# Which weight units of an expert pass stay unsplit, and what the first three prepared units are

## The reference, cut to what matters

```python
def moe_swiglu(h, w_router, w1, w3, w2):
    logits = (h @ w_router).astype(jnp.float32)
    top_logit, top_idx = lax.top_k(logits, TOP_K)      # TOP_K = 2
    gates = jax.nn.softmax(top_logit, axis=-1)
    ...
        return (jax.nn.silu(xblk @ w1[e]) * (xblk @ w3[e])) @ w2[e]
    ...
    return jnp.zeros_like(h).at[tok].add(yb * gate[:, None])
```

## Time and profile before

| | us |
|---|---|
| median of 3 runs | 2702.24 (2699.02 to 2707.3) |
| the profiled execution's own time | 2699.6 |
| its span, first to last instruction | 2697.8 |
| TensorE busy | 2603.4 (97%) |
| TensorE weight load busy | 2052.8 (76%) |
| VectorE busy | 1822.9 (68%) |
| ScalarE busy | 1437.6 (53%) |
| mean granted TensorE clock | 0.988 of full |

### The profile page before, as it was taken

One profiled execution on the slowest core, in us unless ns is written; L12 is line 12 of the kernel. 1 busy time (PEld: TensorE's weight loads), 2 busy tenths in 40 slices (PEclk: granted clock), 3 DMA queues, 4 the chain that ended last, 5 costly groups with the idle time before them and its releaser, 6 DMA issues.

```text
span 2697.8 us, 47127 instructions
## 1 busy us (share of the span) xinstructions
PE 2603.4 (97%) x18358; PEld 2052.8 (76%) x18358; DVE 1822.9 (68%) x2625; ACT 1437.6 (53%) x2065; POOL 0.2 (0%) x4
## 2 busy tenths in 40 slices
PE   8999999999999999999999999999999999999998
PEld 6787777888788888867877897678886666666666
DVE  4876574435422233368666658998989898898887
ACT  6534375223422223255344645777777677777775
POOL 0000000000000000000000000000000000000000
PEclk9999999999999999999999999999999999999998
DMA  7010273324222233210114456999999999999996
GB/s 288 2 50 32 97 268 122 103 101 164 79 94 94 102 107 119 94 47 2 50 63 168 147 186 231 369 405 353 361 356 389 402 402 406 410 400 398 410 402 268
DMA packets 80005, 576.16 MB, mean 214 GB/s; under 512 B 8784, under 2 KB 10192, under 8 KB 10192
## 3 DMA queue, kind: packets, MB, share of 16 engines
q1 hardware_dynamic: 79536, 571.84, 54.5%
q10 hardware_dynamic: 288, 1.74, 0.2%
HBM read 572.49 MB, written 1.05 MB: 213 GB/s over the span
## 4 chain that ended last, share of the span: by engine, by line
PE 78%; DVE 11%; ACT 6%; issue 4%; DMA 1%; DVEq 0%; ACTq 0%; SPq 0%
PE bank L584 74%; DVE weights_low L2785 2%; DVE more_weights_low L2785 2%; PE bank L845 2%; ACT more_weights_high L1630 2%; ACT weights_high L1630 2%; DMA ring<-wstream 1%; ACT arena L1630 1%; PE bank L1266 1%; PE bank L1523 1%; DVE weights_low L2388 1%; DVE arena L2700 1%; PE bank L696 0%; DVE y_rows_low L3128 0%; PE bank L1051 0%
## 5 line engine op out<-in xcount | busy, mean ns | idle before, releaser
L1630 ACT ACTIVATE arena<-bank 128x512 f32<-128x512 f32 (+3 forms) x578 | 275.6, 492 | 765.9 <-PE bank L584 691.9
L1630 ACT ACTIVATE weights_high<-ring 128x1024 fp32r<-128x1024 f32 (+1 forms) x345 | 467.9, 1364 | 253.5 <-PE bank L584 243.1
L2388 DVE TENSOR_TENSOR weights_low<-ring,weights_high 128x1024 fp32r<-128x1024 f32 x220 | 266.8, 1224 | 399.3 <-ACT weights_high L1630 399.3
L584 PE MATMUL bank<-h_low,weights_high 128*128 128x512 f32 (+1 forms) x960 | 346.9, 361 | 0.0
L2785 DVE TENSOR_TENSOR weights_low<-ring,weights_high 128x2048 fp32r<-128x2048 f32 x125 | 285.1, 2287 | 36.9 <-ACT weights_high L1630 36.3
L584 PE MATMUL bank<-arena 64*64 64x64 f32 (+5 forms) x4944 | 267.0, 242 | 15.6 <-DVE arena L2603 4.5
L584 PEld LDWEIGHTS bank<-arena 64*64 64x64 f32 (+3 forms) x4944 | 224.5, 143 | 39.1 <-issue 14.0
L2785 DVE TENSOR_TENSOR more_weights_low<-arena,weights_high 128x2048 fp32r<-128x2048 f32 x87 | 199.1, 2288 | 20.4 <-ACT weights_high L1630 19.1
L584 PEld LDWEIGHTS bank<-h_low,weights_high 128*128 128x128 f32 x960 | 181.7, 189 | 27.5
L584 PE MATMUL bank<-weights_high,tokens_high 128*128 128x512 f32 x544 | 184.7, 427 | 1.0 <-DVEq L2941 1.0
L1630 ACT ACTIVATE weights_high<-arena 128x2048 fp32r<-128x2048 f32 x87 | 166.3, 1911 | 29.4 <-DMA arena<-wstream 17.2
(11 more groups left out here) (342 smaller groups left out, 5119.3 us busy)
## 6 DMA issues: line engine op xcount, KB each, us to landing
ring<-wstream SPq DMA_DIRECT2D x368, 1024.0 KB, 5.7
arena<-wstream SPq DMA_DIRECT2D x171, 1024.0 KB, 7.5
xT<-xin SPq DMA_DIRECT2D x2, 1024.0 KB, 6.2
cn<-consts SPq DMA_DIRECT2D x1, 1576.0 KB, 22.0
sm<-small SPq DMA_DIRECT2D x1, 1568.0 KB, 24.6
sm<-small ACTq DMA_DIRECT2D x1, 1568.0 KB, 11.4
out<-hT SPq DMA_DIRECT2D x2, 512.0 KB, 3.0
cn<-consts ACTq DMA_DIRECT2D x1, 130.0 KB, 2.7
```

The source lines that it names most:

```text
L584: return nc.tensor.matmul(o, lhsT, rhs, start=first, stop=last)
L1630: return nc.scalar.activation(o, i, func, **kw)
L2388: step(vx.tensor_tensor(ring_low[:, u % RING, cols], ring[:, u % RING, cols], wh[:, j % 4, :].bitcast(F32), ALU.subtract), "weights low", j)
```

## The change

Four things are edited.
- In small passes the unsplit units among 0 to 27 are those with q % 4 == 2 (2, 6, ..., 26) in place of q % 4 == 3 (3, 7, ..., 27). Units 33 and 38 stay unsplit. The number of unsplit units, nine, is the same.
- The three units prepared at a boundary ahead of a small pass are its first three split ones: 0, 1 and 3. SyncE loads four units (in place of three) of the pass after the last fixed one before it looks whether there is such a pass.
- Groups 2 and 3 are scattered after pair 3 (with VectorE's `add_last`), and the gates are turned after pair 5.
- `pick_gates` no longer waits for the second gather of the pass before; ScalarE waits for unit 27 to be spent before it copies the gathered tokens.

```diff
-UNSPLIT = [q for q in range(2 * PAIRS) if q % 4 == 3] + [33, 38]
+UNSPLIT = [q for q in range(2 * PAIRS) if q % 4 == 2] + [33, 38]
...
+        def split_units(wide):
+
+            return list(range(MOE_UNITS)) if wide else SPLIT
...
+        def split_here(q, wide):
+
+            return q in split_units(wide)[AHEAD:]
...
-            for q in range(AHEAD):
+            begun = SPLIT[AHEAD - 1] + 1
+            for q in range(begun):
                 load(first, EXPERTS, q)
...
-                        pe.wait_ge(*(here("high", q) if q >= AHEAD else before("next high", q)))
+                    pe.wait_ge(*(here("high", q) if split_here(q, wide) else before("next high", high_turn(q, wide))))
...
-                    if p == 2:
+                    if p == 3:
                         for g in range(2, 4):
                             scatter_last(g)
-                    if p == 4:
+                    if p == 5:
                         pe.wait_ge(*here("gates picked"))
...
-                    if not wide and q in UNSPLIT:
+                    if not split_here(q, wide):
                         book.leave_out(e_scalars)
                         return
...
                 def next_high(q):
 
-                    act.wait_ge(moe_loaded[q], (i + 1) * (16 * MOE_UNITS // MOE_RING) + 16)
-                    act.wait_ge(*here("spent", MOE_UNITS - AHEAD + q if wide else SPLIT[len(SPLIT) - AHEAD + q]))
-                    f(moe_high(q), moe_slot(q)[0], ACT.Copy).then_inc(*tick(e_scalars, kind, "next high", q))
+                    u = split_units(wide_next)[q]
+                    act.wait_ge(moe_loaded[u], (i + 1) * (16 * MOE_UNITS // MOE_RING) + 16)
+                    act.wait_ge(*here("spent", split_units(wide)[q - AHEAD]))
+                    f(moe_high(q), moe_slot(u)[0], ACT.Copy).then_inc(*tick(e_scalars, kind, "next high", q))
...
-                    if p == 4:
+                    if p == 5:
                         act.wait_ge(*here("gates turned"))
...
+                    act.wait_ge(*here("spent", 2 * PAIRS - 1))
                     keep(xh[:, 4 * b:4 * b + 4, 0:slots_next],
...
             def pick_gates(i):
 
-                dve.wait_ge(*in_pass(i - 1, "gathered", 1))
...
-                rest(AHEAD - 1).then_inc(*tick(e_vectors, kind, "low", AHEAD - 1))
+                head = split_units(wide)[AHEAD - 1]
+                rest(head, AHEAD - 1).then_inc(*tick(e_vectors, kind, "low", head))
...
-                    if p in (1, 2):
-                        add_last(2 * p - 2)
-                        add_last(2 * p - 1)
+                    if p in (1, 3):
+                        add_last(p - 1)
+                        add_last(p)
```

More of the change, by code:

```diff
@@ L421, in moe_slot @@
             return (ring[:, r, :], ring_low[:, r, :]) if s < RING else (more[:, s - RING, :], more_low[:, s - RING, :])
+        def split_units(wide):
+            return list(range(MOE_UNITS)) if wide else SPLIT
         def high_turn(q, wide):
-            return q if wide else SPLIT.index(q)
+            return split_units(wide).index(q)
+        def split_here(q, wide):
+            return q in split_units(wide)[AHEAD:]
         def high_before(q, wide):
-            return q - AHEAD if wide else SPLIT[SPLIT.index(q) - AHEAD]
+            return split_units(wide)[high_turn(q, wide) - AHEAD]
         more_high = part("more_weights_high", [P, UW], tile_at(37))
@@ L481, in in_pass @@
             return s, (i + 1) * per_pass(s) + value
-        BOUNDARY = [("y kept", 0), ("y kept", 1), ("gathered low", 0), ("gathered low", 1), ("gathered", 1)] + \
+        BOUNDARY = [("y kept", 0), ("y kept", 1), ("gathered low", 0), ("gathered low", 1)] + \
             [(name, q) for name in ("next high", "next low") for q in range(AHEAD - (name == "next low"))]
@@ L569, in _ @@
                     first = first_unit(j + EXPERTS)
-                    for q in range(AHEAD, MOE_UNITS):
+                    for q in range(begun, MOE_UNITS):
                         load(first, j + EXPERTS, q)
                     first = first_unit(j + (EXPERTS + 1))
-                    for q in range(AHEAD):
+                    for q in range(begun):
                         load(first, j + (EXPERTS + 1), q)
@@ L1549, in expert_pass @@
                                 None if not wide and q in UNSPLIT else
-                                here("low", q) if q >= AHEAD - 1 else before("next low", q))
+                                here("low", q) if high_turn(q, wide) >= AHEAD - 1 else
+                                before("next low", high_turn(q, wide)))
                         if not wide and b == 0 and p >= 2:
@@ L1755, in first_high @@
             def first_high(q):
-                act.wait_ge(moe_loaded[q], 16)
-                f(moe_high(q), moe_slot(q)[0], ACT.Copy).then_inc(*tick(scalars, "first high", q))
+                act.wait_ge(moe_loaded[SPLIT[q]], 16)
+                f(moe_high(q), moe_slot(SPLIT[q])[0], ACT.Copy).then_inc(*tick(scalars, "first high", q))
             for l in range(DEPTH):
@@ L3123, in expert_pass @@
                     dve.wait_ge(*here("next high", q))
-                    rest(q).then_inc(*tick(e_vectors, kind, "next low", q))
+                    rest(split_units(wide_next)[q], q).then_inc(*tick(e_vectors, kind, "next low", q))
                 for n in range(2):
```

## The result

| | before | changed |
|---|---|---|
| median of 4 runs, us | 2702.35 | 2742.11 (2740.73 to 2750.31) |
| ratio, 95% interval | | 1.0152 [1.0133, 1.0172] |
| profiled execution, span | 2697.8 | 2748.5 |
| mean granted clock | 0.988 | 0.981 |

The change makes the kernel 1.5% slower, 40 us. The profiled execution happens to be the longest of the four; where it is used, 8 us of its difference is not in the median. The lines of the changed kernel have moved by some ten (L2785 is now L2796, L3075 L3085, L3082 L3092, ScalarE's helper L1639).

A forecast was written before the change was run, and what follows sets the result against it. It took the order of waits through TensorE, ScalarE and VectorE to decide, with all small-pass resources nearly full. Losses of 20.7 us plus 5 for the clock gave 2725.3 profiled, 2728 median; own range 2712 to 2737, wide range 2703 to 2746.

The forecast's parts named there:

- third rival: Boundary: unit 3's weights land late, its remainder slips 2.5 us in five passes, or the clock falls in all seven: 2740; chance 0.13.
- the clock's term: TensorE's wait before pair 12: granted clock falls in three of seven passes at 1.7 us each, 5 us; bounds 0 and 12.
- the landing: Unit 3's raw weights at the boundary: landed about 2239.7, before the third copy needs them; 1 us later lengthens the pass 1 us.
- Boundary: Start of passes 4 to 8: TensorE's 2.68 us stall at unit 2 and the 1.7 us of clock are gone.
- Period: VectorE's chain over two pairs (four units) takes 10.90 us against 9.75, as the odd pair's copy queues behind small_gate.
- Wait for pair 12: End of the gate part: TensorE stands about 2.3 us for VectorE before turning pair 12.
- Where it goes: Units 28 to 41, behind the gather: they keep their queues, so the pass's shift is kept, no more.
- Everything but the clock: Sum over passes: 12.0 us in passes 4 to 8, 3.3 in pass 3, 5.4 in pass 0, wide passes nothing; together 20.7.
- The faster one: Rival: the boundary stall is simply gone and passes 4 to 8 go down to the DMA bound: 2675; chance 0.12.

The follow-up runs named there:

- e1: Changed kernel, but in odd pairs of small passes ScalarE copies the next split unit before small_gate, VectorE's remainder likewise before small_hidden: 2675.15 us, ratio 0.9902.
- e4: Kernel before, with one order changed: in odd pairs of small passes ScalarE does small_gate ahead of its copy of unit 4m+6: 2781.43 us, ratio 1.0298.
- e9: Changed kernel plus 4 unused 128x256 matmuls on TensorE ahead of the wait for pair 12 in small passes: 2725.68 us, ratio 1.0089.
- e3: Changed kernel, but in small passes TensorE turns pair 12 behind the gather in place of ahead of it: 2722.68 us, ratio 1.0076.
- e10: Kernel before plus 5 unused 128x256 matmuls on TensorE between unit 2's high part and its wait for the remainder: 2694.78 us, ratio 0.9973.
- e2: Changed kernel with only the first unsplit unit moved (2, 7, 11, ..., 27, 33, 38), old queues behind pair 0: 2679.16 us, ratio 0.9919.
- e6: Kernel before with only scatters 2 and 3 moved behind pair 3 and the gates behind pair 5: 2689.28 us, ratio 0.9957.

## Why the prediction was right in sign and too small

The forecast was 26 us slower; it is 40. The time, 2742, lies in the wide range of 2703 to 2746, but above the forecast's own 2712 to 2737 and closest to the third rival's 2740. That the wide range holds it is partly luck, as the clock's term lies outside its own bounds. Nor did the third rival come true: the landing cost 1 us in one pass and not 2.5 in five, and seven falls at its price are 12 us, which with the 20.7 of the rest makes 2735.

- *Boundary.* Stall and clock gone there: right. The remainder of the new third unit was to start 2242.1 - 2236.16 = 5.9 us after unit 0. In pass 5 it starts 6.2 after it; in pass 4 it is 7.1 (2150.99 and 2143.89 in the rows above), where the copy waited for DMA until 2148.42, 4.5 after unit 0. In passes 5 to 8 that copy starts 2.9 to 3.7 after unit 0, by the same timelines, for the 3.5 derived. So the landing was right but for pass 4, and of the third rival 1 us in one pass came true. From unit 0 to the turn of pair 12, passes 3 to 8 take 4.0, 3.5, 3.1, 2.5, 3.0 and 2.4 us longer than before; 3.3 and then five times 2.4 were predicted.
- *Period.* 10.90 predicted, 10.96 measured. The steps of 2.40, 0.59, 2.20 and 0.34 stand in the rows above; 2.97 was 3.01. That TensorE is not in the chain was right (e1 undoes it, e4 makes it).
- *Wait for pair 12.* 2.3 predicted, 2.12 measured. *Where it goes:* kept down to the next pass, right.
- *Everything but the clock.* 20.7 us predicted, that is 2723. The two kernels that keep the clock up in passes 3 to 8 without touching VectorE's order measure 2722.7 and 2725.7, 20.7 and 24.1 over the kernel before as timed beside them. So the sum is right or up to 4 too small. Its parts were each a little small: the profile of e9 has 6.9 in pass 0 (5.4 predicted), 5.0 in pass 3 (3.3) and 2.6 to 3.4 in passes 4 to 8 (2.4), by the distances between `y kept`. The agreement of e3 to a tenth is luck, since it moves the turn of pair 12 as well.
- *The clock: the term that was mis-sized.* I took 1.7 us for a fall, from the old boundary, and three falls: 5. Without the fall 16.4 us are gone (e9 against the changed kernel), which the bounds of 0 and 12 did not hold. Both factors were too small. The price: behind the wait for pair 12 the clock stays down for about 10 us (0.50 in the window from 2225 to 2235, full in the next), at half rate 5 us, while behind the boundary a fall was worth about 1.5 (e10). The number: in the profiled execution it falls in five passes, 3 to 7. Windows of 12 or 13 us around the gather lose, by 1 minus the granted clock, 3.4 us in pass 3, 5.1 in pass 4 and 5.2 in each of passes 5 to 7, some 24 in all; that execution is 8 us longer than the median, which leaves 16. One fall of 1.7 us more is in pass 0 (0.55 from 1692.30 to 1696.00). Pass 8 had a wait of 2.13, no fall, and lost 1.9, against the 2.4 worked out. The wait's length, by which the number was judged, was no guide: see the last section.
- *Rivals.* The faster one was wrong for this kernel, but its price was right: with the queues in order, e1 and e2 give 2675 and 2679 against 2675 forecast. The page "Perfetto Trace Analysis" of the Trainium skill (Identifying the Most-Contended Engine, Optimization Strategy) would close the gaps of the fullest engine first. That is borne out by e2 (2679) and not by the change (2742): the gap closed was the right one, and the same edit opened another on an engine that was 89% busy.

## What to carry to other kernels

When an item is skipped in one of two in-order queues that feed each other, look at what the skipped item stood between: here it kept a copy ahead of an instruction that waits for the other engine, and the work itself did not change. Walk one period of the two queues with start-to-start times; it gave 10.90 against 10.96, where busy shares showed nothing. And price a stall by what runs behind it as well: when the clock fell, 2.7 us of idle TensorE ahead of large matmuls cost about 1.5 us more, and 2.1 us ahead of a gather of small ones about 5 more.

## What was not expected of the hardware

After a wait of 2.12 us the granted clock stayed at 1.2 GHz while TensorE was busy 10.00 of 10.00 us, first with the gather (32 records of 128x64, 6.10 us for 3.71), and rose only after several 128x512 matmuls of units 28 and 29. Behind the boundary stall of 2.68 us of the kernel before, where 128x512 matmuls follow at once, it was down for about 3.4 us (0.57 over 4.00 us). Why it stays down through the gather was not tested: small matmuls and the idle time before them come together here. The length of the wait alone did not decide whether it fell at all. Boundary waits of 2.64 to 3.54 us were followed by a fall five times of five in the kernel before and three times of five in e6. The same wait in pass 0 was followed by 0.55 in the changed kernel (2.10 us) and by 1.00 in e9 (2.09 us). A wait of 1.91 us in pass 3 of the kernel before left the clock at 1.00, while one of 1.79 us in pass 0 of e1 was followed by 0.66 (1687.40 to 1690.40). What else decides was not tested.
